# FFN up projection by Strassen's scheme over pairs of spans, with the branch and out units moved ahead

## The reference, cut to what matters

```
proj  = rmsnorm(x) @ w_in                    # mixer inputs and gates
h_m, h_a = mlstm(...), swa_attend(...)
mixed = ga * (h_m @ w_a) + gb * (h_a @ w_b)  # "branch"
x     = x + mixed @ w_out                    # "out"
u     = rmsnorm(x) @ w_up                    # "up", 1024 x 5632
c     = b_conv + sum over 3 taps of w_conv[tap] * u shifted by tap
h     = gelu(c[:, :2816]) * c[:, 2816:]
x     = x + h @ w_down                       # "down", 2816 x 1024
y     = rmsnorm(x)
```

## Time and profile before

| | |
|---|---|
| median of 3 runs | 2914.91 us |
| span of the profiled execution, first to last instruction | 2912.9 us |
| TensorE busy | 98% |
| VectorE, ScalarE, GpSimd busy | 61%, 47%, 23% |
| granted TensorE clock, mean | 0.994 of full speed |
| DMA, mean | 148 GB/s |

### The profile page before, as it was taken

The page is one execution under the profiler, slowest core; times in us unless marked ns, Lnnn a source line. Parts: engine busy times, 40 slices in busy tenths (PEclk is TensorE's granted clock), DMA queues, the critical chain, the costliest instruction groups (busy, mean ns, idle before and its releaser), DMA issues.

```text
span 2912.9 us, 43961 instructions
## 1 busy us (share of the span) xinstructions
PE 2862.1 (98%) x16514; PEld 2738.3 (94%) x16514; DVE 1772.0 (61%) x2545; ACT 1373.9 (47%) x2376; POOL 662.6 (23%) x943
## 2 busy tenths in 40 slices
PE   8999999999999999999999999999999999999998
PEld 8888898989988999999999999999999999999997
DVE  4212267676777566655587655876558765577665
ACT  3212235454555455544465444654446544455454
POOL 2111022111112112112242122321223212134232
PEclk9999999999999999999999999999999999999999
DMA  5644365556655373543434444345443454434434
GB/s 183 202 134 130 105 207 180 187 178 230 185 159 158 113 229 101 170 129 111 148 117 158 153 139 146 108 159 158 140 149 113 143 158 142 122 114 121 136 116 93
DMA packets 257077, 431.32 MB, mean 148 GB/s; under 512 B 39458, under 2 KB 171106, under 8 KB 256866
## 3 DMA queue, kind: packets, MB, share of 16 engines
q1 hardware_dynamic: 254754, 428.37, 47.3%
q10 hardware_dynamic: 2112, 0.13, 0.0%
HBM read 363.68 MB, written 65.77 MB: 147 GB/s over the span
## 4 chain that ended last, share of the span: by engine, by line
PE 64%; DVE 1%; ACT 0%; issue 0%; DVEq 0%; ACTq 0%
PE f_ps L2054 42%; PE f_ps L2059 21%; PE f_st L2066 0%; DVE f_rinv L2282 0%; DVE both_low L2404 0%; ACT f_wh L2116 0%; DVE f_wl L2261 0%; DVE both_high L2286 0%; DVE f_xl L2295 0%; DVEq L2517 0%; ACT L2125 0%; ACT f_rinv L2125 0%; ACT f_xh L2154 0%; DVE both_low L2396 0%; ACT f_hh L2146 0%
## 5 line engine op out<-in xcount | busy, mean ns | idle before, releaser
L2261 DVE TENSOR_TENSOR f_wl<-both_high,f_wh 128x1024 fp32r<-128x1024 f32 (+2 forms) x460 | 544.8, 1184 | 143.3 <-ACT f_wh L2116 137.9
L2054 PE MATMUL f_ps<-f_xh,f_wh 128*128 128x416 f32 x1760 | 618.0, 351 | 3.0 <-DVE f_xl L2295 3.0
L2054 PE MATMUL f_ps<-f_xl,f_wh 128*128 128x416 f32 x1760 | 618.6, 351 | 0.0
L2116 ACT ACTIVATE f_wh<-both_high 128x1024 fp32r<-128x1024 f32 (+2 forms) x460 | 442.0, 964 | 286.7 <-PE f_ps L2059 283.8
L2059 PE MATMUL f_ps<-f_xh,f_wl 128*128 128x416 f32 x1760 | 367.8, 351 | 0.0
L2054 PEld LDWEIGHTS f_ps<-f_xh,f_wh 128*128 128x128 f32 x1760 | 330.1, 188 | 10.5 <-DVE f_xl L2295 4.7
L2314 DVE SCALAR_TENSOR_TENSOR both_high<-both_high,f_taps 128x416 f32<-128x416 f32 (+2 forms) x264 | 154.3, 598 | 296.6 <-ACT both_high L2174 296.4
L2054 PEld LDWEIGHTS f_ps<-f_xl,f_wh 128*128 128x128 f32 x1760 | 330.8, 188 | 3.9 <-issue 0.6
L2059 PEld LDWEIGHTS f_ps<-f_xh,f_wl 128*128 128x128 f32 x1760 | 329.9, 188 | 2.3
L2172 ACT ACTIVATE both_high<-f_ps 128x416 f32<-128x416 f32 (+2 forms) x264 | 116.9, 460 | 389.9 <-PE f_ps L2059 389.8
L829 PE MATMUL pp<-gxh,gwh 128*128 128x416 f32 x792 | 290.9, 367 | 2.4 <-DVE gxl L778 1.3
(11 more groups left out here) (325 smaller groups left out, 4976.3 us busy)
## 6 DMA issues: line engine op xcount, KB each, us to landing
both_high<-in_w_up SPq DMA_DIRECT2D x220, 512.0 KB, 3.7
both_high<-in_w_dn SPq DMA_DIRECT2D x120, 384.0 KB, 3.1
both_low<-in_w_gate SPq DMA_DIRECT2D x80, 512.0 KB, 4.7
both_high<-in_w_br SPq DMA_DIRECT2D x40, 512.0 KB, 3.9
both_high<-in_w_out SPq DMA_DIRECT2D x40, 512.0 KB, 3.6
gate_rows<-gsgo SPq DMA_DIRECT2D x98, 208.0 KB, 3.5
both_low<-in_w_mix SPq DMA_DIRECT2D x12, 1024.0 KB, 7.9
both_low<-in_w_mix SPq DMA_DIRECT2D x20, 512.0 KB, 5.4
```

The costliest lines, as they stand in the source:

```text
L2054: pe.matmul(ps[n][:, 0:TB], wh[s][:, (col + k) * P:(col + k) * P + P], x[:, k0 + k, :], start=(k == 0 and x is xhi), stop=False)
L2116: act.activation(wh[v % WS][:, 0:w], raw[s][:, 0:w], ACT.Copy).then_inc(ev("w_hi"), 1)
L2261: dve.tensor_tensor(wl[n][:, 0:w], raw[s][:, 0:w], wh[n][:, 0:w].bitcast(F32), ALU.subtract).then_inc(ev("w_lo"), 1)
```

## The change

All branch and out units come first, span by span. The normed x and the x after the mixer are stored to DRAM (`span_out`, `normed_out`) and read back. The FFN then works on three pairs of spans, 696, 696 and 688 columns wide; a half of a pair (w) is 348 or 344 columns. For each tile r, the a and g channels, the two halves of the 1024 inputs and the two halves of the pair make a 2x2 by 2x2 block product, which is done by seven products over 4 k-tiles (`PRODUCTS`, units "q") instead of eight. The sums of inputs are made once for each pair (`prep_sums`, `prep_high`, `prep_lows`); the four sums of weights for each tile are made on VectorE in the first pair (`weight_sum`), stored to DRAM and read back in the two others. ScalarE and VectorE combine the seven results out of four PSUM banks (0 to 3), with the products 4 to 6 added in PSUM to those of 0, 2 and 3. The taps, gelu, product and split work on the whole pair at once (`w2` columns), and the product of the halves moves from GpSimd to VectorE. Weights are split in chunks of 512 columns (`QUAD`) in a ring of six, up to five chunks ahead. A down unit does both halves of the pair (two products of w columns), in six parts; its banks are 4 to 6. The final norm works on 696 columns, in two halves.

```diff
+PRODUCTS = (("a11", "b11", 0), ("s2", "t2", 1), ("s3", "t3", 2), ("s1", "t1", 3), ("a12", "b21", 0), ("a22", "t4", 2), ("s4", "b22", 3))
+    for b in range(SPANS):
+        units += [("branch", b, i) for i in range(KT)] + [("out", b, i) for i in range(KT)]
+    for p in range(PAIRS):
...
+            stop = FT if part + 2 >= len(PARTS) else BEGIN[part + 1] + 1
+            for r in range(at, stop):
+                units += [("q", FT * p + r, j) for j in range(NQ)]
+            at = stop
+            units += [("down", p, KT * part + o) for o in range(KT)]
...
     @block.tensor
-                product(v, q, 0, KT, xh, xl, 0, "x_lo" if i == b == 0 else None)
+                if i == 0:
+                    wait(pe, "c11_ready", n)
+                elif i == 1:
+                    wait(pe, "v_ready", n)
+                elif i == 2:
+                    wait(pe, "c21_ready", n)
+                elif i == 3:
+                    wait(pe, "c12_ready", n)
+                elif i == 4:
+                    wait(pe, "a_ready", n + 1)
+                elif i == 5:
+                    wait(pe, "u3_ready", n + 1)
+                else:
+                    wait(pe, "c22_ready", n + 1)
+                product(ps[bank][:, 0:w], FIRST[v], 4, lambda k: xth[:, j, k, 0:w], lambda k: xtl[:, j, k, 0:w],
+                        start=i < 4, stop=i == 1 or i > 3)
...
+        def final_sum(p):
+            for s in range(2):
+                wait(pe, "frt_ready", 2 * p + s)
+                pe.matmul(stp[:, 0:w], ones, facc[:, WIDE * s:WIDE * s + w], start=True, stop=True).then_inc(ev("fst_done"), 1)
...
     @block.vector
+        def third(n):
+            dve.wait_ge(ev("mm_done"), group_done(n, 2))
+            dve.wait_ge(ev("v_ready"), n + 1)
+            for t, f in pieces(pair_of(n), u[1], 1):
+                ins = dve.tensor_tensor(t, f(ps[2]), f(value), ALU.add)
+            ins.then_inc(ev("u3_ready"), 1)
...
+            if kind == "q":
+                if i == 2:
+                    difference(b)
+                elif i == 3:
+                    third(b)
+                elif i == 4:
+                    c22(b)
+                elif i == 6:
+                    c21(b)
+            names = post.get(v, ())
+            for name, n in names:
+                if name == "c12":
+                    c12(n)
+            for n, w in sums_at.get(v, ()):
+                weight_sum(n, w)
+            for e in range(split, split_until(v)):
+                w_low(e)
+            for name, n in names:
+                if name == "taps1":
+                    taps_of(n, 1)
+                elif name == "taps0":
+                    taps_of(n, 0)
+                elif name == "product":
+                    product(n)
+                elif name == "low":
+                    g_low(n)
```

More of the change, by code:

```diff
@@ new lines, with banks @@
+AHEAD_W = RING - 1
+DOWN_AT = [v for v, u in enumerate(PLAN) if u[0] == "down"]
+DOWN_N = {v: i for i, v in enumerate(DOWN_AT)}
+def banks():
+    bank, before, count, at = [], [], [0] * 8, 0
+    for v, (kind, b, i) in enumerate(PLAN):
+        mine = []
+        if kind in ("branch", "out"):
+            for _ in range(2 if kind == "branch" else 1):
+                mine.append(at % BANKS_C)
+                at += 1
+        elif kind == "down":
+            d = 2 * DOWN_N[v]
+            mine = [4 + (d + s) % BANKS_D for s in range(2)]
+        bank.append(mine)
+        before.append([count[m] for m in mine])
+        for m in mine:
+            count[m] += 1
+        if kind != "down":
+            closed = list(count)
+    return bank, before, closed
@@ L1833, in tiles_of, with behind, posts @@
[L1833 to L1845, removed]
+def behind(n):
+    return AT["q", n, NQ - 1] + 1
+def posts():
+    out = {}
+    for n in range(FT * PAIRS):
+        v = behind(n)
+        steps = (("c12", "taps1"), ("taps0",), ("product",), ("high",), ("low",))
+        if PLAN[v][0] == "down":
+            steps = (("c12", "taps1"), ("taps0",), ("product", "high"), ("low",))
+        for k, names in enumerate(steps):
+            out.setdefault(v + k, []).extend((name, n) for name in names)
+    return out
@@ L1882, in ffn_phase @@
[L1882 to L1901, removed]
@@ L2181, in _ @@
         h_high(0, 0)
         w_high(0)
+        w_high(1)
         for k in range(1, KT):
             h_high(0, k)
-        w_high(1)
+        for e in range(2, FIRST[2]):
+            w_high(e)
         gates(0, 0)
+        split = FIRST[2]
         for v, (kind, b, i) in enumerate(PLAN):
-            w_high(v + WS - 1)
-            q = BANK[v]
+            for e in range(split, split_until(v)):
+                w_high(e)
+            split = max(split, split_until(v))
+            if kind == "q" and i == 1:
+                first_copy(b)
+            if kind == "q" and i == 5:
+                c11(b)
+            for name, n in post.get(v, ()):
+                if name == "taps0":
+                    scaled(n, 0)
+                if name == "product":
+                    gelu(n)
+                if name == "high":
+                    g_high(n)
+            if kind == "q" and i == 6:
+                scaled(b, 1)
```

1148 lines of the change are left out of this document (709 added, 439 removed).

## The result

| | before | after |
|---|---|---|
| median, 4 runs each | 2914.86 us | 2947.48 us (2945.41 to 2951.84) |
| span of the profiled execution | 2912.9 | 2943.1 |
| granted TensorE clock, mean | 0.994 | 0.982 |

The ratio is 1.0115, with a 95% interval of 1.010 to 1.0129: slower by 33 us. The forecast was 61 us faster (2854, range 2805 to 2905). Rival B had the sign and, with 2933 (18 us slower), about half of the size, but not the mechanism, as the experiments show.

What follows compares the result with a forecast made beforehand. TensorE's matmuls were taken to bound the FFN phase, with VectorE deciding pair 0. An ideal span of 2793 plus 15 (pair 0), 28 (starts), 8 (ends), 3 (DMA), 5 (unseen) and 2 around it gave 2854 us, range 2805 to 2905.

Steps and rivals of the forecast that it cites:

- Rival B: VectorE, all tiles: instructions tied by waits pay whole lengths, exceeding 13.25 us a tile; 2933 us; chance 0.11.
- C: All matmuls: narrower ones get no shorter as weights reload each time; 3120 us, milder by the skill's slope; chance 0.01.
- E: Up products: the seven-product scheme doesn't cut the columns; chance 0.
- VectorE in steady tiles: Product tiles: pair 0 runs at VectorE's pace, 14.2 us against 13.25, 11 us over 12 tiles; pairs 1 and 2 fit.
- A: Whole phase: everything hides, totals, norms and prepares cost a third and pair 0 nothing; 2810 us; chance 0.15.
- Starts of pairs 1 and 2: First tiles of pairs 1 and 2: final norm work, GpSimd totals and lower clock cost 14 us each, 28 together.
- term (a): Pair starts: `final_sum` holds TensorE while ScalarE splits, evacuates, loads the table and takes the first root; 2.6 us.
- (c): Pair starts: GpSimd's 16 totals delay `tail`, for which ScalarE's `first_copy` and then the first taps wait; 3 us.
- term (b): Pair starts: inverse and eight scalings put 11.5 us more on VectorE in tiles 1 to 3; 5.3 us late.
- Ends of pairs 0 and 1: Down part 5: preparing the next pair beside adds and splits on VectorE costs 4 us each, 8 together.
- Branch and out: Branch and out units: 372 us; pair 0's preparing hides beside span 4's out units, mixed-row waits add 4 us.
- D: Pair 0: the clock falls to 1.2 GHz, five such tiles undo the gain, half its tiles give 3000 us; chance 0.03.

Runs made afterwards that it cites:

- e1: Changed kernel with ScalarE's scaling of the first half's conv input moved ahead of product 0's evacuation in product unit 1: 2911.28 us.
- e2: Changed kernel with pair 0's four weight sums per tile formed on only 32 of 512 columns (results wrong): 2924 us.
- e10: e7 with the final norm's inverse of pairs 0 and 1 formed on 8 of 348 columns (outputs wrong): 2888 us.
- e7: e1 plus GpSimd totals before heads, second column sum in its own bank, inverse in two instructions, scalings over tiles 2 to 4, residual loaded in halves: 2897 us.
- e3: Changed kernel with ScalarE's third copy in a pair's preparing issued one unit later, behind that unit's weight splits: 2928 us.
- e6: e3 plus pair 0's tiles prepared one unit earlier and the last mixed row taken last in each span's first out unit: 2915 us.
- e11: e6 and e7 together on the changed kernel, final norm's sum and root in unit 4: 2864.41 us, ratio 0.983 to the kernel before.
- e5: Changed kernel with pair 0's product of the gelu and the other half back on GpSimd: 2954 us.

## Why the prediction was wrong, by its steps

- **Matmul spacing: right, at the upper bound.** The forecast had 158 ns for 348 columns, at most 159.4; twelve take 1.9125 us on the mean of pair 1's steady tiles, 159.4. For 344 it is 157 for 156. That is some 10 us in all, at the edge of the bounds given. C and E are out with it. So is the milder form of C, by the slope of the Trainium skill ("TensorE: Matmul & The Clock Gate", section "Back-to-back issue gap"): this trace disagrees with it for 348 columns too.
- **VectorE in steady tiles: the durations right, the step wrong.** "12 tiles of pair 0 lose 0.95: 11 us", "pair 2: 12.6 against 13.1", so nothing. The sum took VectorE's instructions as a row with no gaps and asked only whether its length fits in a tile. ScalarE was given no order of its own. With `first_copy` ahead of `scaled` VectorE stood idle ahead of the taps 56 times, 0.8 us on the mean and 1.4 at the longest. Pairs 0 and 2 can't absorb that; pair 1 can (11.7 in 13.4). e1 gave back 34 us of the up units' 43. The work alone costs pair 0 about 6 (e1 and e2), less than the forecast's 11.
- **Rival B: wrong mechanism.** It had VectorE pay 0.735 and 0.95 for each split and tap. Then e1, which takes no work away, could not have given 34 us. The steady tiles of pair 1 lose nothing, and the distances on VectorE are those of the earlier trace rows. Its term for pair 1 was also too big by its own figures: 13.4 against 13.25 is 0.15 a tile, not 0.3. A, with everything hidden, is out by the 96 us of waits.
- **Starts of pairs 1 and 2: near for pair 1, 6 us short for pair 2, and partly right in the terms.** Forecast 14 each. Pair 1 lost 15.6 (311.8 us for 296.2 of matmuls), pair 2 about 20 beside its steady idle time (309.3 in e1 for 289.6). In term (a) the sum waits once more, for GpSimd's totals (2.8 us), which stood behind `head`; (c) had put this delay on `tail`. Of term (b) the inverse is borne out: e10 gave 7 us in the up units for the two. The eight scalings were only spread (e7), and no run shows their share.
- **Ends of pairs 0 and 1: mis-sized.** Forecast 4 each, measured 12 and 11. The 4 doesn't follow from the forecast's own terms: 7.5 + 7 + 3.8 of VectorE against 15.1 is 3.2, and 1.3 with the 1.9 that it may be late. In e3 two whole preparations (9.2 us) ran in part 5's time, not 7.5 us of them, and VectorE was busy for 20.6 us there. Six and four of the loss were again two engines waiting by turns (e3). Also left out was down part 0 of pairs 1 and 2, 4 and 2 us (5 and 3 in e1): the residual's load waits for the last scaled rows and then stands ahead of the down weights (e7).
- **Branch and out: left out.** "prepared beside the out units of span 4" was priced at nothing. The eight out units of span 4 have 36 us of matmuls and took 54.1, and VectorE was busy for 41.9 of these, more than the 36, with the same turn-taking on top: the last four out units, up to pair 0's first product, took 33.9 us for 18.1, 16 lost. The five starts of out units were priced at 1 each by one row; they cost 1.3 to 3.1. e3 and e6 gave back 21.6 of 28.
- **The clock** fell at these places and nowhere in steady tiles, so D is out; what the lower level costs is part of the terms above, as it went where the waits went. In after the phase had 98 us of it, the tail's 23 among them, in e11 53, before 28. The forecast priced it at 3 us a pair start and nowhere else; by the estimate above it cost some 25 us in after and 13 in e11.
- **Tail:** 23.9 for 22. **DMA:** the refill of the single role buffers, which was feared, made one wait of 1.8 us; the residual's load, which was not thought of, 4 and 2. ScalarE also waited 22.3 us in 29 times for the loads of the other down weights (the kernel before has one such wait, 2.9 us), and nothing of that reached TensorE in down parts 1 to 3, which took 30.2 to 30.7 us as without a wait.

Once the orders are mended the forecast's sum holds to 10 us: e11 has 378.8, 922.4, 516.9 and 21.9 us for 372, 919, 507 and 22. The forecast gave the price of the change in a kernel whose queues had been rearranged for it. That the terms agree so well is in part luck: in e11 the ends and the spacing cost more than forecast, and the pair starts less. What it asked of the wait chain ("`third` ends at about 8.1 with the waits for ScalarE's scaled copy") was one engine's order, and the other's was not written out beside it.

## What to carry to other kernels

- When units get shorter and two engines hand work to each other, write out both orders side by side, with each wait. A busy share of 69% says nothing on a step that is late in a fixed order: 45 us of idle time stood ahead of one line here.
- On an in-order engine, put an instruction that waits for a late event behind those that are ready. Moving one line gave 36 us, moving another 19, and neither took work away.
- Look at where things begin and end (pair starts, last parts, first units). Over half of the loss was there, and the lower clock came only there.

## What was not expected of the hardware

- A two-input VectorE instruction beside a GpSimd two-input one does not just get slower: a pair of sums took 2.78 us beside a product of 1.68 us. The Trainium skill ("SBUF — State Buffer", section "Who interferes with whom") has the later of the two wait, and the trace agrees: the second sum began behind the product and ended 0.5 us after it. The prediction set the 1.22 us of a 1024-wide split against this rule, but that split began at 1511.96, ahead of GpSimd's product at 1512.19, so by the rule the product is the one to wait. GpSimd pays too. Its product on 416 columns took 1838 ns on the mean in the kernel before, on 696 columns in e5 1694. Its totals on 348 columns take 1155 ns on the mean in pair starts, on 344 columns in the tail's stretch 925. That a busy VectorE beside it is the cause is likely by the rule, and not shown by a run of its own:

```profile
L2851 POOL TENSOR_TENSOR f_nrm<-f_nrm 128x348 f32<-128x348 f32 x28 | 31.5, 1155 | 2.2 <-ACT f_nrm L2475 2.2
...
L2851 POOL TENSOR_TENSOR f_nrm<-f_nrm 128x344 f32<-128x344 f32 x14 | 12.6, 925 | 2.7 <-ACT f_nrm L2475 2.6
```

- One short wait can be enough for the lower clock, with TensorE at work before and behind it. At 1143.14 us of after it had waited 1.85 us for the mixed rows; from 1144.0 the granted clock was at its lower level, 1.2 GHz, for 3.4 us, and matmuls on 416 columns started 0.35 us apart, not 0.19. A second wait of 1.85 us, at 1296.19, was followed by the same; the two others of this length were not. In the start of pair 1 the mean was 0.87; in e11, with fewer waits, the same stretch is at 0.98:

```profile
1867.00:1942.00 75.00, 66.60 (x395) 64.18 (x395) 66.40 (x100) 43.04 (x73) 22.57 (x28) 0.98 0.44 141
```
